# Normalizing the sums of eight tiles in another order: scales right behind moments, rows weighed elsewhere, turned columns split an iteration later

## The reference

```python
for layer in range(DEPTH):                      # DEPTH = 2
    mix = ab_mixer(...) if layer % 2 == 0 else c_mixer(...)
    x = layer_norm(DEEPNORM_ALPHA * x + mix, ln_gain[layer, 0], ln_bias[layer, 0])
    ffn = hier_moe(x, ...)                      # top-1 group, then top-2 experts in it
    x = layer_norm(DEEPNORM_ALPHA * x + ffn, ln_gain[layer, 1], ln_bias[layer, 1])

def layer_norm(x, g, b):
    mu = mean(x); var = mean((x - mu) ** 2)
    return (x - mu) * rsqrt(var + 1e-5) * g + b
```

## Time and profile before

| | us |
|---|---|
| median of 3 runs | 2438.29 |
| lowest and highest run | 2435.85, 2438.32 |
| the profiled execution's own time | 2434.3 |
| span of its profile | 2432.0 |
| PE busy | 2318.8 |
| DVE busy | 1787.7 |
| ACT busy | 1369.7 |
| POOL busy | 272.3 |
| middle stage, first sum on PE to the projections behind it | 1134.15 to 1200.07 |
| end stage, first sum on PE to the end of the span | 2387.81 to 2432.0 |

### The profile page before, as it was taken

One profiled execution on the slowest core, in us unless ns is written; L12 is line 12 of the kernel. 1 busy time (PEld: TensorE's weight loads), 2 busy tenths in 40 slices (PEclk: granted clock), 3 DMA queues, 4 the chain that ended last, 5 costly groups with the idle time before them and its releaser, 6 DMA issues. The chain is left out here.

```text
span 2432.0 us, 34076 instructions
## 1 busy us (share of the span) xinstructions
PE 2318.8 (95%) x12892; PEld 1892.7 (78%) x12892; DVE 1787.7 (74%) x2512; ACT 1369.7 (56%) x1670; POOL 272.3 (11%) x243
## 2 busy tenths in 40 slices
PE   8999998989999999998899999998979999999996
PEld 6767886877888888886677777776868888888883
DVE  4565557568999999997555455556579999999997
ACT  3454446026777777775344444444037777777774
POOL 0000000001212111111400000000012112211104
PEclk9999999989999999999999999999989999999999
DMA  4110004228999999998211111105049999999986
GB/s 127 27 31 27 27 10 124 113 96 346 390 387 376 387 383 385 388 389 321 93 45 44 40 38 38 38 36 176 35 173 392 395 396 398 391 378 381 373 340 256
DMA packets 155501, 534.36 MB, mean 220 GB/s; under 512 B 39584, under 2 KB 79544, under 8 KB 106184
## 3 DMA queue, kind: packets, MB, share of 16 engines
q1 hardware_dynamic: 136208, 498.45, 54.2%
q0 software_dynamic: 18496, 33.60, 3.6%
q10 hardware_dynamic: 632, 0.10, 0.0%
HBM read 515.21 MB, written 50.41 MB: 233 GB/s over the span
## 5 line engine op out<-in xcount | busy, mean ns | idle before, releaser
L360 DVE TENSOR_TENSOR arena<-arena,arena 128x2048 fp32r<-128x2048 f32 (+1 forms) x458 | 957.0, 2119 | 65.6 <-ACT arena L1937 50.3
L1937 ACT CAST arena<-arena 128x2048 fp32r<-128x2048 f32 x384 | 716.5, 1918 | 131.4 <-PE psum L1656 115.5
L1656 PE MATMUL psum<-arena,arena 128*128 128x512 f32 x3072 | 732.3, 394 | 0.1
L1656 PEld LDWEIGHTS psum<-arena,arena 128*128 128x128 f32 x3072 | 568.5, 188 | 114.1 <-issue 0.4
L657 PE MATMUL psum<-arena,arena 128*128 128x512 f32 x2016 | 505.5, 401 | 6.3 <-DVE arena L360 5.6
L657 PEld LDWEIGHTS psum<-arena,arena 128*128 128x128 f32 x2016 | 369.1, 189 | 100.2 <-issue 11.4
L1667 PE MATMUL psum<-arena,arena 128*128 128x512 f32 x1536 | 359.9, 390 | 2.8 <-DVE arena L360 2.8
L1667 PEld LDWEIGHTS psum<-arena,arena 128*128 128x128 f32 x1536 | 287.9, 188 | 64.5 <-DVE arena L360 4.6
L360 DVE TENSOR_TENSOR arena<-psum,arena 128x512 fp32r<-128x512 f32 (+1 forms) x186 | 160.6, 871 | 110.6 <-ACT arena L782 55.3
L799 ACT ACTIVATE arena<-arena,arena 128x640 f32<-128x640 f32 (+4 forms) x192 | 120.0, 626 | 204.9 <-DVE arena L897 154.5
L1188 PE MATMUL psum<-arena,arena 128*128 128x512 f32 x768 | 190.6, 404 | 9.5 <-ACT arena L356 6.9
(11 more groups left out here) (179 smaller groups left out, 1667.3 us busy)
## 6 DMA issues: line engine op xcount, KB each, us to landing
arena<-in_moe_w_gate SPq DMA_DIRECT2D x128, 1024.0 KB, 9.1
arena<-in_moe_w_up SPq DMA_DIRECT2D x128, 1024.0 KB, 7.9
arena<-in_moe_w_down SPq DMA_DIRECT2D x128, 1024.0 KB, 7.1
arena<-expert_rows SPq DMA_DIRECT2D x32, 512.0 KB, 10.8
x_rows<-arena SPq DMA_DIRECT2D x24, 512.0 KB, 2.6
arena<-in_c_w_in SPq DMA_DIRECT2D x24, 512.0 KB, 9.6
arena<-x_rows SPq DMA_DIRECT2D x24, 512.0 KB, 8.2
arena<-in_x SPq DMA_DIRECT2D x16, 512.0 KB, 6.7
```

Source lines behind the costliest of these rows:

```text
L360: return eng.tensor_tensor(tile, src, high.bitcast(F32), ALU.subtract)
L1656: mm = pe.matmul(bank(o), cs[:, c * P:(c + 1) * P], ws[:, c * FF:(c + 1) * FF], start=(k == 0 and c == 0), stop=(k == 2 and c == CH - 1))
L1937: act.copy(w_hi[w][:, cols], self.raw[w][:, cols]).then_inc(hi_ready[w], 1)
```

## The change

On the engines' lists of Combine the order is changed, and no instruction is added or dropped.

- DVE, middle stage: `finish(t)` comes right behind `moments(t)`. Before, it came behind the next tile's `add`. In the end stage it comes between the two halves of the next tile's `add`, which is cut in two for this.
- ACT, middle stage: `norm(t)` comes an iteration sooner, so that the weighing of tile 3 and up stands behind the norm of one tile more. In the end stage tiles 2, 3 and 4 are weighed ahead of the first root, and the others four tiles ahead.
- ACT and DVE, middle stage: `keep_tile(0)` moves from iteration 3 to iteration 4, tiles 1 and 2 to iteration 5, tile 3 stays in iteration 6, tile 4 in iteration 7. On DVE `split_w(2)` moves from iteration 1 to iteration 3.
- PE, middle stage: tiles 0 to 4 are summed ahead of the first turn, before it was 0 to 3.

```diff
+                weighed_early, lead_of_rows = (5, 4) if last else (3, 2)
+                def keep_after(t):
+                    return () if last else {4: (0,), 5: (1, 2), 6: (3,), 7: (4,)}.get(t, ())
...
@@ scalar
-                    self.scale_rows(act, 2)
+                    for t in range(EARLY, weighed_early):
+                        self.scale_rows(act, t)
                     for t in range(TILES):
-                        if t >= 1:
-                            act_norm(act, t - 1)
-                        if 1 <= t < TILES - 2:
-                            self.scale_rows(act, t + 2)
+                        act_norm(act, t)
+                        if weighed_early <= t + lead_of_rows < TILES:
+                            self.scale_rows(act, t + lead_of_rows)
                         if not last and t == 1:
-                            act.wait_ge(added, 2)
                             split_w(2)
-                        if t >= 3 and not last:
-                            keep_tile(t - 3)
-                    act_norm(act, TILES - 1)
+                        for k in keep_after(t):
+                            keep_tile(k)
@@ vector
                     for t in range(TILES):
-                        add(dve, chain, t)
-                        if t >= 2:
+                        add_first(dve, chain, t)
+                        if last and t >= 2:
                             finish(dve, chain, t - 1)
+                        add_rest(dve, t)
                         moments(dve, chain, t)
-                        if t == 0:
+                        if not last or t == 0:
                             finish(dve, chain, t)
-                        if not last and t == 1:
+                        if not last and t == 3:
                             split_w(2)
-                        if t >= 3 and not last:
-                            keep_tile(t - 3)
-                    finish(dve, chain, TILES - 1)
+                        for k in keep_after(t):
+                            keep_tile(k)
+                    if last:
+                        finish(dve, chain, TILES - 1)
@@ tensor
-                    for t in range(TILES if last else 4):
+                    for t in range(TILES if last else 5):
                         sum_up(pe, t)
...
                     for t in range(4):
                         turn_tile(t)
-                        sum_up(pe, t + 4)
+                        if t + 5 < TILES:
+                            sum_up(pe, t + 5)
```

More of the change, by code:

```diff
@@ L2327, in act_norm, with add_first @@
                         norm_apply(act, rows[t], t, shared.index(t), scale_ready, normed)
-                def add(dve, chain, t):
+                def add_first(dve, chain, t):
                     dve.wait_ge(summed, t + 1)
@@ L2335, in add, with add_rest @@
                                                             op0=ALU.mult, op1=ALU.add))
+                def add_rest(dve, t):
                     if t < MADE:
```

## The result

The changed kernel takes 2449.49 us, the median of 5 runs (2448.67 to 2452.38), beside 2438.32 us, the median of 5 runs of the kernel before. The ratio is 1.0048, with a 95% interval of 1.0033 to 1.0063. That is 0.5% slower, some 12 us (8 to 15).

What follows compares the result with a forecast made beforehand. PE was taken as the bound, busy 2318.8 of 2432.0 us, with time lost only where it waits or at the end. Middle +12.2 and end +1.1 gave +13.3 us on 2438.29, said as 2452; range 2446 to 2458.

Steps and rivals of the forecast that it cites:

- Step (a): Middle stage, DVE: finish directly behind moments exposes ACT's root, 0.33 us a tile, now also for tiles 1 to 6.
- Step (b): Middle stage: ACT runs tile 2's root late, so DVE waits 1.6 us in place of 0.33.
- Step (c): Middle stage: tile 3's rows are weighed later, so DVE waits 4.8 us for PE's sum, 2.9 if the clock stays up.
- Step (d): Middle stage: low parts behind finish make DVE wait for ACT, 2.9 us twice, 1.6 more and 1.9; together 9.3 us.
- The ledger: Count of DVE's waits up to tile 3's low part (middle) and tile 7 (end): 12.2 and 1.1 us later.
- Step (f): Middle stage, DVE: the moved split of the weight takes 1.2 us in place of 3.01, so -1.8 us; other bound 0.
- the term "removed": End stage: DVE's two waits for the sums of tiles 4 and 6 go, 2 x 2.08 = 4.2 us.
- The rival of a lower clock behind the new waits: Middle stage: clock also drops in later turns and projections, and a POOL pass hits the split; 2455 to 2459, chance 0.15.
- The rival that something behind the stage gives the loss back: Behind the middle stage something had to wait anyway, so only the end stage's loss remains; 2439, chance 0.06.

Runs made afterwards that it cites:

- PE kept busy: Changed kernel with 16 thrown-away matmuls added on PE ahead of tile 3's sum in the middle stage; ratio 1.0036 to the kernel before.
- Finish put back: Changed kernel with the middle stage's finish on DVE behind the next tile's sum again, and ACT's norm and tile 3's weighing moved back too; ratio 0.9991 to before.
- rows weighed sooner: Changed kernel with the middle stage's tile 3 weighed behind tile 0's norm as before, and tiles 4 to 7 one norm sooner; ratio 1.0033 to before.
- the split at 3: Kernel before with only DVE's split of the weight in the middle stage moved from iteration 1 to 3; ratio 0.9984 to the kernel before.
- the end stage alone: Middle stage of the kernel before with the end stage of the changed kernel; ratio 0.9994 to the kernel before.
- weighing rows ahead there: Kernel before with, in the end stage, tile 3 weighed ahead of the first root and tiles 4 to 7 one norm sooner; ratio 0.9968 to before.
- the middle stage alone: Changed kernel's middle stage with the end stage of the kernel before; ratio 1.0055 to the kernel before.

## Why the prediction was right

The time, 2449.49, lies 2.5 us below the 2452 said, and its steps can be checked one by one. The first projections were to start near 1187.8 and started at 1188.89, in an execution whose stage began 0.85 us later.

Step (a), exposed roots: 0.27 us idle for each, priced 0.33 from start to start. Step (b), tile 2's root: 1.55 us idle, priced 1.6. Step (c), tile 3's sum: PE idle 4.16 us ahead of it, DVE 5.00 us, priced 4.8 (its own terms, 2.9 and 1.7 for the clock, add up to 4.6). It is shown by taking it away (6.0 us of waits with step (b)) and the part of the clock by itself (the wait 1.7 us shorter with PE kept busy). Step (d), low parts behind finish: 2.81, 2.82, 1.45 and 1.78 us, priced 2.9, 2.9, 1.6 and 1.9. Finish put back takes all four steps away at once, and A is that of before within 0.3 us; rows weighed sooner takes (b) and (c) away and leaves (a) and (d), with A 5.8 us above before. The middle stage was to be 12.2 us longer and A is 12.5, B 12.7. The ledger had no term for the clock at the start of the stage, where DVE waited 0.44 us less for the first sum after the change than before and 0.16 us more for the second. Without it A would be 12.8 us longer, and that the number came out closer is luck.

Step (f) was wrong as a cause, though its figure came true: the split took 1.22 us, and the ledger of DVE's time needs this entry. But I read it as 1.8 us gained by the move. Moved alone, it gained nothing in the execution profiled (41.43 against 41.39), because the split at iteration 1 covered PE's sums, and it would gain some 1 us by an estimate where PE's clock rises sooner. In the changed kernel DVE waits at tile 3 with or without it, so what counts there is only that it stands behind that wait (iteration 3, 1.22 us on the path) or ahead of it (iteration 2, free: 1.14 us less).

The Trainium skill's rule on the shared port (SBUF — State Buffer, "SBUF: two separate sides"), which I set beside the 3.01 us, is borne out in both directions. With the split started first, POOL's instruction is the one stretched. This is POOL's timeline in the kernel with finish put back, where the split starts at 1157.60:

```profile
1155.51 2.39 POOL L1031 TENSOR_TENSOR arena<-arena,arena 128x1024 f32<-128x1024 f32 x1
1157.86 3.36 POOL L1027 TENSOR_TENSOR arena<-arena,arena 128x1024 f32<-128x1024 f32 x1
```

3.36 us in place of 2.4 for the L1027 that found the split under way, and 1.38 us for the split, whose first 0.3 us fell in the end of L1031.

The end stage was priced at +1.1 us and measures +1.0 between the two profiles, step by step: 3.25 us for the first root, priced 3.3 (it was 1.87 in one later execution and 4.22 in another, as tile 4's rows landed earlier or later), 0.34, 0.67 and 0.34 us for the others. But the term "removed", twice 2.08 us, was sized on one execution, and it was a favourable one. In the kernel with the split at 3, whose end stage is that of before, the same two waits are:

```profile
2411.51 1.22 DVE L2350 SCALAR_TENSOR_TENSOR arena<-arena,psum 128x1024 f32<-128x1024 f32 x1 [3.74 <-PE psum L2328]
...
2422.88 1.23 DVE L2350 SCALAR_TENSOR_TENSOR psum<-arena,psum 128x1024 f32<-128x1024 f32 x1 [3.77 <-PE psum L2328]
```

and its C is 47.51. PE had idled 3.21 and 2.43 us ahead of these sums, as before, but the granted clock then fell, to 0.75 in 2408 to 2412 and 0.60 in 2416 to 2420:

```profile
2408.00:2412.00 4.00, 4.00 (x11) 2.00 (x9) 0.49 (x1) 0.56 (x2) 3.92 (x2) 0.75 0.50 204
2416.00:2420.00 4.00, 3.45 (x5) 1.45 (x6) 3.00 (x7) 2.88 (x5) 3.92 (x3) 0.60 0.00 0
```

So the end stage before costs 44.2 us (in two of its three profiles) or up to 47.5, by the execution, and the change takes away the wait that is hit by it. That fits the end stage alone being 0.9994 of before and not above 1, the 8 us won by weighing rows ahead there against 3.5 us in one pair of profiles, and the measured 12 us, below my 13.3. How often either case comes was not measured, so the share of it in these numbers stays argued.

The rival of a lower clock behind the new waits came true in part (the granted clock was 0.60 in 1162 to 1166, 0.62 in 1170 to 1174 and 0.50 in 1178 to 1182), and hardly on the path: these sums were ready before DVE asked. Only at tile 2's turned groups did it cost something. DVE waited 1.29 and 0.16 us there, about the 1.6 us that I had counted for another reason, and PE turned the tile in 1.95 us. In the kernel with the middle stage alone the same turn took 1.22 us, at a granted clock of 1.00, and DVE waited 0.89 us. So 0.6 us of the 1.45 was the clock. The rival that something behind the stage gives the loss back is out: B is longer by as much as A.

## What to carry to other kernels

Where engines hand work around with lists in fixed order, an early issue of the small step (the scale right behind the moments) is only early if the engine that answers is free, and it takes away the work that hid the answer; count for each moved instruction what stands behind it on its own engine and who asks for that. Ask of an instruction that is slow whether something else is being waited for anyway: the split of 3 us looked like 1.8 us to win and gave nothing when it was moved alone. And weigh ahead only what has landed: of the two tiles brought ahead of the first root in the end stage, tile 3 was free (0.27 us waited for the root with tile 3 alone ahead), and tile 4 held the root up by 3.3 us.

## What the runs showed of the hardware that was not expected

The same gap on PE, at the same place of the same code, has two prices. After 3.21 us idle the sum of tile 4 in the end stage ran at the full granted clock in the kernel before (DVE's wait 2.08 us) and at 0.75 in another execution with the same end stage (3.74 us). The Trainium skill (TensorE: Matmul & The Clock Gate, "Part 1: The HAM clock gate") says that the place at which the clock rises under sustained matmuls varies from run to run. The starts of the middle stage agree (from 4.0 to 8.0 us behind the first matmul the granted clock was 1.00 before and 0.78 with the split at 3). The two executions of the end stage show the same of its fall behind one gap, so that a price read from one profile is one of two. The middle stage has such a pair as well: behind 3.46 us idle PE turned tile 2 in 1.95 us in the changed kernel, and behind 3.49 us in 1.22 us in the kernel with the middle stage alone. Filling the gap of 4.16 us ahead of tile 3's sum with matmuls that nobody needs kept the granted clock at 1.00 and took 1.7 us off DVE's wait for that sum.
